# Low weight parts written over the raw tiles, 18 gelu slots, spread steps over 20 tiles, and a third output projection on split weights

## The reference, cut to what matters

```
u   = rms_norm(x) @ w_in_2 + b_in_2            # conv channels, k, v, q
a   = conv_group(...)                          # 1024 channels: gated conv, layer norm, silu
b   = swa_group(q, k, v)                       # 16 heads of 64, window 128, softmax with sinks
h   = x + concat(a, b) @ w_out_2               # the third output projection
xn  = rms_norm(h)
q   = xn @ peer_w_q                            # 8 heads, top 16 of 16 x 16 key pairs: 128 slots a token
gates = softmax(vals)
out = h + sum_e gates[e] * gelu(xn . peer_u[e]) * peer_v[e]     # over the chosen ones of 16384 experts
```

## Time and profile before

| | before |
|---|---|
| median of three runs | 3288.03 us |
| the profiled execution | 3288.3 us |
| its span, first to last instruction | 3285.9 us |
| mean granted TensorE clock | 0.972 of full speed |
| TensorE, VectorE, ScalarE, GpSimd busy | 95%, 55%, 49%, 19% |
| loads of weights | 475 of 1 MB, 154 GB/s over the span |

### The profile page before, as it was taken

How to read it: one execution, slowest core, us unless ns; L and a number is a source line. 1 busy time by engine, 2 the same in 40 slices (tenths; PEclk the granted TensorE clock), 3 DMA queues, 4 the chain that set the end, 5 groups by cost and what they waited for, 6 DMA issues and landing times.

```text
span 3285.9 us, 64081 instructions
## 1 busy us (share of the span) xinstructions
PE 3132.1 (95%) x25170; PEld 3030.3 (92%) x25170; DVE 1820.2 (55%) x3306; ACT 1606.3 (49%) x2575; POOL 630.4 (19%) x275
## 2 busy tenths in 40 slices
PE   7999998999999999869999978999998899999998
PEld 7999998999899898658899978999998899999998
DVE  4555545645444459571477787544447755554444
ACT  4766765566677532471344424444443444444443
POOL 3333332444344333100244400000000000000000
PEclk9999998999999899979999989999999999999999
DMA  5333332444433344213455523555553355555554
GB/s 202 128 140 140 135 140 109 169 166 166 148 134 137 119 159 144 100 52 141 168 183 181 181 95 129 179 187 184 189 182 128 121 187 181 189 180 183 187 184 136
DMA packets 72273, 506.38 MB, mean 154 GB/s; under 512 B 7904, under 2 KB 10592, under 8 KB 11232
## 3 DMA queue, kind: packets, MB, share of 16 engines
q1 hardware_dynamic: 71584, 503.09, 43.1%
q10 hardware_dynamic: 576, 1.72, 0.2%
HBM read 502.69 MB, written 2.10 MB: 154 GB/s over the span
## 4 chain that ended last, share of the span: by engine, by line
PE 89%; DVE 6%; ACT 3%; issue 1%; DMA 0%; SPq 0%; DVEq 0%; ACTq 0%
PE bank L436 13%; PE bank L438 13%; PE bank L437 13%; PE bank L2035 7%; PE bank L2033 7%; PE bank L2034 7%; PE bank L449 6%; PE bank L1828 6%; PE bank L1830 6%; PE bank L1829 6%; DVE e_col L1922 1%; DVE c_acc L1215 1%; PE bank L1817 1%; PE bank L678 1%; DVE e_row L1918 1%
## 5 line engine op out<-in xcount | busy, mean ns | idle before, releaser
L413 ACT ACTIVATE whi<-raw 128x1024 fp32r<-128x1024 f32 x866 | 911.3, 1058 | 1102.7 <-PE bank L438 493.3
L420 DVE TENSOR_TENSOR wlo<-raw,whi 128x1024 fp32r<-128x1024 f32 x652 | 790.7, 1225 | 426.8 <-ACT whi L413 425.9
L420 POOL TENSOR_TENSOR wlo<-raw,whi 128x1024 fp32r<-128x1024 f32 x214 | 569.8, 2663 | 1159.6 <-ACT whi L413 1154.0
L2035 PE MATMUL bank<-e_coef_hi,wlo 128*128 128x256 f32 x2048 | 574.5, 281 | 0.0
L2033 PE MATMUL bank<-e_coef_hi,whi 128*128 128x256 f32 x2048 | 573.4, 280 | 0.0
L2034 PE MATMUL bank<-e_coef_lo,whi 128*128 128x256 f32 x2048 | 572.8, 280 | 0.0
L436 PE MATMUL bank<-xa_hi,whi 128*128 128x272 f32 (+1 forms) x1808 | 535.5, 296 | 0.5 <-DVE wlo L420 0.4
L438 PE MATMUL bank<-xa_hi,wlo 128*128 128x272 f32 (+1 forms) x1808 | 526.9, 291 | 0.0
L437 PE MATMUL bank<-xa_lo,whi 128*128 128x272 f32 (+1 forms) x1808 | 524.8, 290 | 0.0
L436 PE MATMUL bank<-xb_hi,whi 128*128 128x256 f32 (+1 forms) x1536 | 441.1, 287 | 8.6 <-DVE f_qg L964 6.1
L1828 PE MATMUL bank<-xb_hi,whi 128*128 128x256 f32 x1536 | 438.5, 286 | 1.2 <-DVE hT L2080 1.2
(11 more groups left out here) (383 smaller groups left out, 4677.6 us busy)
## 6 DMA issues: line engine op xcount, KB each, us to landing
raw<-in_w SPq DMA_DIRECT2D x251, 1024.0 KB, 4.8
raw<-in_v SPq DMA_DIRECT2D x128, 1024.0 KB, 5.3
raw<-in_u SPq DMA_DIRECT2D x96, 1024.0 KB, 4.8
hT<-in_hT SPq DMA_DIRECT2D x4, 544.0 KB, 8.5
out<-hT SPq DMA_DIRECT2D x8, 256.0 KB, 2.8
r_keys<-in_keys ACTq DMA_DIRECT2D x1, 1024.0 KB, 5.6
c_mask<-in_masks ACTq DMA_DIRECT2D x1, 320.0 KB, 2.9
params<-in_params SPq DMA_DIRECT2D x1, 238.5 KB, 2.6
```

The costliest lines, as they stand in the source:

```text
L413: act.activation(whi[:, (2 * t.q + half) % 4, :], raw[:, t.q, half * 1024:(half + 1) * 1024], ACT.Copy).then_inc(w_hi_done, 1)
L420: eng.tensor_tensor(wlo[:, slot, :], raw[:, t.q, half * 1024:(half + 1) * 1024], whi[:, slot, :].bitcast(F32), ALU.subtract).then_inc(w_lo ...
L2035: last = te.matmul(ps, lo, e.coef_hi[:, s % 2, :], start=False, stop=(final and kk % 2 == 1))
```

## The change

`wlo` becomes four whole tiles that lie at the address of `raw` (both declarations start at the same place), so a low part overwrites the raw weights that it was made from. Every load now waits for TensorE's last use of tile n - 4. The 16 KB a partition that `wlo` held go to `e.act`, which has 18 slots. The spread steps go over 20 tiles, two or one a tile; hidden and gelu run beside them into the 18 slots, and the gating follows the last step, up to five a tile. The first 32 tiles of each group are written out; each up tile has a bank of its own out of four. The third output projection takes split weights, low half 0 on VectorE and 1 on GpSimd, and its input is split inside the window attention: a copy into `c.cm` or `c.mm`, a high part on ScalarE and a low part on VectorE for each of 16 tiles. The first tile of that projection is split in slot 9, its low halves both on GpSimd.

```diff
-NATIVE = T_PEERQ - T_CONV
+NATIVE = T_WOUT - T_CONV
+N_ACT = 18
...
         sq2 = tensor(ctx, "sq2", [P, 2, L])
+        with ExitStack() as st:
+            wlo = tensor(st, "wlo", [P, 4, D], F32R)
         raw = tensor(ctx, "raw", [P, 4, D])
...
-        wlo = tensor(ctx, "wlo", [P, 4, D // 2], F32R)
...
-                e.act = tensor(s2, "e_act", [P, 2, SEQ])
+                e.act = tensor(s2, "e_act", [P, N_ACT, SEQ])
...
-            eng.tensor_tensor(wlo[:, slot, :], raw[:, t.q, half * 1024:(half + 1) * 1024],
-                              whi[:, slot, :].bitcast(F32), ALU.subtract).then_inc(w_lo_done[half], 1)
+            eng.tensor_tensor(wlo[:, t.q, at], raw[:, t.q, at], whi[:, slot, :].bitcast(F32),
+                              ALU.subtract).then_inc(w_lo_done[half], 1)
...
-                    if base == T_WOUT:
-                        project_fp32(te, Tile(base, i, s), x, n)
-                    else:
-                        project(te, Tile(base, i, s), x, slice(0, n))
+                    project(te, Tile(base, i, s), x, slice(0, n))
...
         def swa_scalar(act, ch):
             for s in range(NSLOT + 6):
+                if s == NSLOT - 1:
+                    split_hi(act, Tile(T_SWK, 0, s).next())
...
+                if s - 2 in CONV_SLOTS:
+                    k = CONV_SLOTS.index(s - 2)
+                    act.wait_ge(S.cm, k + 1)
+                    act.activation(xa[0][:, k, 0:SEQ], c.cm[:], ACT.Copy).then_inc(x_hi_done, 1)
                 j = s - 7
...
+                j = s - 8
+                if 0 <= j < NQ:
+                    act.wait_ge(S.m, j + 1)
+                    act.activation(xa[0][:, CONV_T + j, 0:SEQ], c.mm[:], ACT.Copy).then_inc(x_hi_done, 1)
...
+            def lo_part(tile_k, src):
+                xcount[0] += 1
+                ve.wait_ge(x_hi_done, SPLITS[T_BOUT] + xcount[0])
+                ve.tensor_tensor(xa[1][:, tile_k, 0:SEQ], src, xa[0][:, tile_k, 0:SEQ].bitcast(F32),
+                                 ALU.subtract).then_inc(x_split, 1)
...
                     ve.tensor_tensor(c.qr[:], proj_ps(tq, SEQ), rinv[:, 0:SEQ], ALU.mult).then_inc(evacuated, 1)
+                if s - 2 in CONV_SLOTS:
+                    lo_part(CONV_SLOTS.index(s - 2), c.cm[:])
...
-                    ve.tensor_copy(xn2[:, CONV_T + j, :], B_RO[:, SEQ:2 * SEQ]).then_inc(S.m, 1)
+                    ve.wait_ge(x_split, SPLITS[T_BOUT] + xcount[0])
+                    ve.tensor_copy(c.mm[:], B_RO[:, SEQ:2 * SEQ]).then_inc(S.m, 1)
...
+                j = s - 8
+                if 0 <= j < NQ:
+                    lo_part(CONV_T + j, c.mm[:])
...
         def swa_pool(po, ch):
             for s in range(NSLOT):
+                if s == NSLOT - 1:
+                    for half in range(2):
+                        split_lo(po, Tile(T_SWK, 0, s).next(), half)
...
+        STATIC_UP = 32
+        def up_ps(q):
+            return bank[U_BANKS[q % 4]][:, 0:SEQ]
...
             k = j - UP_FIRST[g_]
-            return range(k * STEPS_A_TILE, (k + 1) * STEPS_A_TILE) if 0 <= k < STEPS // STEPS_A_TILE else ()
+            upto = lambda k: min((8 * k + 4) // 5, STEPS)
+            return range(upto(k), upto(k + 1)) if k >= 0 else ()
+        def up_plan(g_):
...
+                gates = range(gated, min(gated + 5, act) if last < j < end else act if j == end else gated)
...
+                while j >= UP_FIRST[g_] and hid < j and (hid < N_ACT + 2 or hid - N_ACT - 2 < gated) and hid - 2 < act:
+                    hids.append(hid)
...
+            for j, (gates, hids, _, rest) in enumerate(up_plan(g_)):
+                steps = steps_of(g_, j)
+                if g_ == 0:
+                    for q in steps_of(g_, j - 1):
+                        multiply_kept(ve, q)
+                if j or g_ == 0:
+                    for q in steps[:1]:
                         operands(ve, g_, q)
...
+                if j < STATIC_UP and (g_ or j >= UP_FIRST[0]):
                     both_lo(ve, Tile(T_U[g_], j // 4, j % 4).next())
+                if j == last + 1:
+                    ve.wait_ge(spread_in, STEPS * (g_ + 1))
+                for k in gates:
+                    gated(ve, g_, k)
+                for k in hids:
                     hidden(ve, g_, k)
+                if j or g_ == 0:
+                    for q in steps[1:]:
+                        operands(ve, g_, q)
...
-            weights(4, T_CONV + 4, w_tile, split)
-            weights(T_CONV + 4, T_PEERQ + 4, w_tile, used)
-            weights(T_PEERQ + 4, TILES, w_tile, split_late)
+            weights(4, TILES, w_tile)
...
-            out_vector(ve, ch, OUT[2], ())
+            out_vector(ve, ch, OUT[2], (0,))
...
-            out_pool(po, ch, OUT[2], (0, 1))
+            out_pool(po, ch, OUT[2], (1,))
```

More of the change, by code:

```diff
@@ L242, in build @@
         innermost = ExitStack()
-        with ExitStack() as st:
-            xn2 = tensor(st, "xn2", [P, KT, SEQ])
         xa = (tensor(innermost, "xa_hi", [P, KT, L], F32R), tensor(innermost, "xa_lo", [P, KT, L], F32R))
@@ L547, in body @@
                                          at3(hT, j - 1, cols), ALU.add).then_inc(evacuated, 1)
-                    if base != T_WOUT and splits_next(base, j):
+                    if splits_next(base, j):
                         for half in halves:
@@ L1778, in slots_scalar @@
             act.activation(e.slot_gate, bank[4][:, 0:SEQ], ACT.Copy).then_inc(slots_in, 1)
-        AHEAD = 12
         S_BANKS = (bank[3], bank[4])
-        UP_BANKS = (2, 7, 5, 6, 0, 1)
-        FLUSHED_AT = {b: n for n, b in enumerate((2, 3, 4, 7, 5, 6, 0, 1))}
-        def up_bank(j):
-            return UP_BANKS[j // 2] if j < AHEAD else UP_BANKS[j % 4]
-        def up_ps(j):
-            half = j % 2 if j < AHEAD else 0
-            return bank[up_bank(j)][:, half * SEQ:(half + 1) * SEQ]
+        U_BANKS = R_BANKS
@@ L1801, in late_of @@
-        def late_of(g_, j):
-            start = UP_FIRST[g_] + STEPS // STEPS_A_TILE
-            done = lambda i: 0 if i < start else min(4 * (i - start + 1), i)
-            return range(done(j - 1), done(j))
+            upto = lambda k: min((8 * k + 4) // 5, STEPS)
+            return range(upto(k), upto(k + 1)) if k >= 0 else ()
+        def up_plan(g_):
+            last = max(j for j in range(STATIC_UP) if steps_of(g_, j))
+            end = STATIC_UP if N_UP[g_] == STATIC_UP else STATIC_UP - 1
+            plan, hid, act, gated = [], 0, 0, 0
+            for j in range(end + 1):
+                gates = range(gated, min(gated + 5, act) if last < j < end else act if j == end else gated)
+                gated = gates.stop
+                hids, acts = [], []
+                while act < hid and (act < N_ACT or act - N_ACT < gated):
+                    acts.append(act)
+                    act += 1
+                while j >= UP_FIRST[g_] and hid < j and (hid < N_ACT + 2 or hid - N_ACT - 2 < gated) and hid - 2 < act:
+                    hids.append(hid)
+                    hid += 1
+                    while act < hid and (act < N_ACT or act - N_ACT < gated):
+                        acts.append(act)
+                        act += 1
+                rest = range(gated, j if j == end else gated)
+                gated = rest.stop
+                plan.append((gates, hids, acts, rest))
+            assert hid == act == gated == end
+            return plan
@@ L1833, in up_tensor @@
         def up_tensor(te, ch, g_):
-            for j in range(16):
+            for j in range(STATIC_UP):
                 if j == UP_FIRST[0] and g_ == 0:
@@ L1887, in up_scalar @@
                     act.wait_ge(coef_split, SEG * g_)
+                for k in acts:
+                    gelu(act, g_, k)
                 for q in steps_of(g_, j):
                     spread_in_of(act, g_, q)
-                for k in late_of(g_, j):
-                    gelu(act, g_, k, k % 2)
+            if N_UP[g_] == STATIC_UP:
+                return
             def body(i):
@@ L1903, in body @@
                         break
-            with act.Fori(4, N_UP[g_] // 4) as i:
+            with act.Fori(STATIC_UP // 4, N_UP[g_] // 4) as i:
                 body(i)
@@ L1911, in operands @@
             now = slice(q * STEP, (q + 1) * STEP)
-            if g_ == 0 and q >= 2:
-                multiply_kept(ve, q - 2)
-            else:
-                need(ve, spread, at - 1)
+            need(ve, spread, at - 1)
             ve.tensor_tensor(pairs(e.one[:, b, :, :]), keys(g_ * SEG, SEG), per_token(e.slots[:, 1, now, :], SEG),
@@ L2005, in body @@
                         break
-            with ve.Fori(4, N_UP[g_] // 4) as i:
+            with ve.Fori(STATIC_UP // 4, N_UP[g_] // 4) as i:
                 body(i)
@@ L2095, in _, with weights @@
                 sp.dma_start(raw[:, q, :], w_in[q]).then_inc(w_loaded[q], 16)
-            def split(n):
-                for half in range(2):
-                    sp.wait_ge(w_lo_done[half], n - 3)
             def used(n):
```

(7 more changed lines are left out.)

125 lines of the change are left out of this document (53 added, 72 removed).

## The result

The kernel after takes **3214.39 us** (median of 4 runs, 3213.99 to 3218.16) against 3288.45 (3287.46 to 3289.05) of the kernel before, measured beside it: ratio 0.9775, 95% interval 0.9761 to 0.9789. The profiled execution took 3213.99 us, span 3212.1, against 3288.3 and 3285.9. The forecast was 3226, 11.6 us too long.

The account below looks back on a forecast made before the run. TensorE, busy 95% of the span, bounds the kernel; time comes only from its idle, lower clock or needless passes. 3288.3 - 27.6 - 25.7 - 20.0 + 11 = 3226.0, said as 3226; range 3208 to 3250.

Parts of the forecast that it names:

- Group 1, 27.6: Group 1's up phase: fewer spread steps a tile recover 30.1 us lost, less 2.5 for start and close calls.
- Group 0, 25.7: Group 0's up phase: fewer spread steps a tile recover 41.7 us lost, less 16 us that stay.
- The queue sum: Group 0's two-step tiles: VectorE needs 6.95 us, TensorE wants operands at 6.41; 0.6 us wait in each of 12 tiles.
- Projection, 20.0: Third output projection on split weights: 16 tiles of 5.68 us plus 1.9 for a slow first tile, against 112.8.
- Rival D: New projection: GpSimd's half makes VectorE the bound, tile 6.05 us, +6 us, 3232; chance 0.06.
- Attention, +11: Window attention's ring of engines without idle: splitting the projection's input there costs 11 us, bounds 5 to 18.
- The price of slot 9: Attention slot 9: ScalarE's high split and GpSimd's low halves holding up VectorE cost 5.5 us, not ScalarE's 2.5.
- Part 3, 0: Low parts written over raw tiles, loads issued later: same instruction size, loads still covered, cost 0.
- the cover of the loads: Later loads, wanted 17.0 us after issue: the latest needs 12.7 us, a usual one 9; cover 4 us.
- Rival C: Attention's ring absorbs its additions, cost 5 not 11, or group 0 waits 8 us less: 3212; chance 0.07.
- B: Both groups' up phases: second operand set stays late, 24 tiles x 1.5 = 36 us instead of 8: 3254; chance 0.13.
- E: Loads come late for tiles held by TensorE, slower, deciding from some 13 us latency in a down phase; chance 0.03.

Follow-up runs that it names:

- the two runs: Kernel after with GpSimd's low parts of the projection's first tile held back, 3215.09 us; kernel after with that tile's whole split at the attention's end, 3213.33 us.
- part 3 alone: Kernel before with low parts over raw tiles and loads waiting for TensorE's last use, 3278.73 us; same plus an unused tensor keeping other addresses, 3278.01 us.

## Why the prediction was right, and where it was not

Its sum was 3288.3 - 27.6 - 25.7 - 20.0 + 11.

- **Group 1, 27.6:** measured 29.0. The 2.5 us left for the start and for close calls were 1.2, at the start. No slack by the count, and hardly any needed: two-step tiles take 7.13 to 7.19 against a wanted 7.14.
- **Group 0, 25.7:** measured 26.2. The queue sum said 0.6 us a two-step tile and 6.3 for the first; nine of the twelve take 7.88, 0.74 over 7.14, and the first step tile took 12.93, 5.8 over the 7.14 of its two steps. TensorE's waits for e_col were 9.9 us, not the 13 named, and 15.5 us stayed in place of 16. Right by its own steps, and the run with the changed order confirms the cause: taking the low part out from between the two sets took 10.3 of them away.
- **Projection, 20.0:** measured 19.9, with a first tile of 7.58 at clock 0.73 (named: 7.6) and 5.68 from the second on. Rival D is out: GpSimd stretches one operation a tile, xb_lo, and root<-root,sq beside it stays as it was:

```profile
L544 DVE SCALAR_TENSOR_TENSOR xb_lo<-hT,params,xb_hi 128x256 fp32r<-128x256 f32 x16 | 38.3, 2391 | 1.1 <-ACT xb_hi L512 0.7
...
L553 DVE TENSOR_TENSOR root<-root,sq 128x256 f32<-128x256 f32 x15 | 6.2, 413 | 0.0
```

- **Attention, +11:** measured +10.5. Slot by slot: slot 8 0 (named 0.15); slot 9 5.3 (5.5); slots 10 and 11 0.6 and 0.7 (0.76 each); 12 and 13 1.0 each (1.1); slot 14 with the end 2.0 (1.4). The price of slot 9, ScalarE's share plus VectorE's work held by GpSimd, is what the two runs measured as 1.5 to 2.1 and 3.2; two operations were caught, not one. The Trainium skill, SBUF — State Buffer, Who interferes with whom, on the exclusive shared port pair: these rows agree, each operation that was caught ended within 0.3 us of a GpSimd half.
- **Part 3, 0:** this is the step that failed. "The instruction keeps its size and writes where it reads ... 0" looked at VectorE's instruction alone, and that did stay (1225 ns as a mean before, 1228 after and in the two kernels of part 3 alone). The gain of 9.9 us comes from the changed layout and, where the rows show it without a change of clock, lies in TensorE's stream. A changed SBUF layout had not been given a term, nor a bound in the range; 3214 is still inside, 6 us above the lower end, and that is luck as far as this term goes. The second half of part 3's reasoning, the cover of the loads, held, and one tile further than needed.

The range's upper end doesn't follow from its own bounds: gains of 26 and 12 and a cost of 18 give 3268, not 3245. Nothing rests on it here.

Rival C's time, 3212, is nearer to the result than the forecast's, yet its mechanism isn't what happened: the ring cost 10.5 and not 5, and group 0 lost its 16 us. B, D and E did not occur; the run with late loads tests E. With a tile less of cover a load would decide, by the forecast's own count, from some 13.3 - 5.7 = 7.6 us instead of 13.3, still beyond the 4.8 to 5.3 us of a usual load, and that kernel takes 3219, 5 us more.

## What to carry to other kernels

When two engines work through queues that meet tile by tile, write down the sum of the slower one's queue between the instruction that frees a buffer and the one that fills it: it forecast the tiles to within 0.2 us here, and it also named the fix (what the other engine is waiting for goes ahead of what it needs last). A GpSimd instruction with SBUF inputs is priced by what it holds up on VectorE, and here moving it in the ring only moved that price. And a change that moves tensors in SBUF is two changes: run the layout alone before its gain is put down to the edit.

## What had not been expected of the hardware

The place of a tensor in SBUF is worth 10 to 12 us of 3288 here, with the same instructions in the same order: 3277.2 against 3289.6 by one moved allocation, nothing (3290.5 against 3290.7) by changing the high and low tensors round. The part of it that repeats shows as 29.64 against 29.76 us for the same 239 matmuls at granted clock 1.00. Head periods at the lower clock are 7, 7 and 9 of 15 in the three slow layouts and 4 to 7 in the others; these counts overlap, and nothing shows that the layout sets them. The cause is open. The nearest statement is in the Trainium skill, SBUF — State Buffer, Who interferes with whom, by which only the shared port pair causes contention. That pair cannot be all of it here: in these heads VectorE's and GpSimd's busy times are the same in both kernels (15.84 and 11.17 us against 15.86 and 11.24), and what got shorter is TensorE's.
